# A hybrid decoder step on one core: two HGRN heads to a level's matmul, eight places for the last sequence's value pages

## The reference

```
f_t = lb + (1 - lb) sigmoid(z_t)
S_t = diag(f_t) S_{t-1} + (1 - f_t) i_t^T
o_t = S_t^T q_t
```

## Time and profile before

| what | value |
|---|---|
| median of three runs | 2284.1 us |
| the profiled execution's own time / its span | 2280.88 us / 2279.3 us |
| PE busy | 2039.0 us (89%) |
| DVE busy | 1647.4 us (72%) |
| ACT busy / POOL busy | 503.4 us (22%) / 199.6 us (9%) |
| moved by DMA | 356.42 MB, 156 GB/s on average |
| TensorE clock granted | 0.943 on average |

### The profile page before, as it was taken

The page is one execution under the profiler, slowest core; times in us unless marked ns, Lnnn a source line. Parts: engine busy times, 40 slices in busy tenths (PEclk is TensorE's granted clock), DMA queues, the critical chain, the costliest instruction groups (busy, mean ns, idle before and its releaser), DMA issues.

```text
span 2279.3 us, 30198 instructions
## 1 busy us (share of the span) xinstructions
PE 2039.0 (89%) x8954; PEld 1056.7 (46%) x8954; DVE 1647.4 (72%) x3478; ACT 503.4 (22%) x1248; POOL 199.6 (9%) x390
## 2 busy tenths in 40 slices
PE   6899899988899889687879998999999998999974
PEld 3445445544444445344445554455445554555340
DVE  2588777776777777577578877888688878888531
ACT  1233233433343334233101110111101111011100
POOL 0000121211111111110200000000000000000000
PEclk9999999999999999798979999999999999999966
DMA  6254455634443343543455553555355544555353
GB/s 216 98 163 159 158 195 187 195 138 143 154 143 121 120 134 122 188 176 113 157 166 170 172 167 129 172 171 180 102 190 168 173 162 136 178 164 171 112 177 117
DMA packets 167798, 356.42 MB, mean 156 GB/s; under 512 B 21040, under 2 KB 25920, under 8 KB 167648
## 3 DMA queue, kind: packets, MB, share of 16 engines
q1 hardware_dynamic: 136144, 248.80, 33.2%
q0 software_dynamic: 31504, 105.80, 13.8%
HBM read 322.52 MB, written 32.00 MB: 156 GB/s over the span
## 4 chain that ended last, share of the span: by engine, by line
PE 37%; DVE 9%; DMA 3%; SPq 2%; issue 2%; ACT 0%; DVEq 0%; ACTq 0%
PE PS L729 17%; PE PS L809 8%; PE PS L841 4%; PE PD L500 2%; DVE Kt L1306 2%; DVE sc L1311 2%; DMA Kt<-in_cache_k_dram 2%; DMA Vt<-in_cache_v_dram 1%; SPq L2025 1%; SPq L2018 1%; PE PO L861 1%; PE PO L862 1%; PE PS L867 1%; PE PS L914 1%; PE PT L743 1%
## 5 line engine op out<-in xcount | busy, mean ns | idle before, releaser
L399 PE MATMUL PT<-W,xT 128*128 128x512 f32 x960 | 436.2, 602 | 1.2 <-ACT xT L969 1.1
L1306 DVE TENSOR_TENSOR Kt<-Kt,qb 128x1024 f32<-128x1024 f32 x256 | 311.9, 1218 | 38.6 <-DMA Kt<-in_cache_k_dram 38.1
L1311 DVE TENSOR_REDUCE sc<-Kt 128x16 f32<-128x1024 f32 x256 | 312.2, 1219 | 8.0
L399 PEld LDWEIGHTS PT<-W,xT 128*128 128x128 f32 x960 | 178.7, 194 | 194.6 <-issue 192.6
L729 PE MATMUL PS<-W,xbuf 128*128 128x512 f32 (+1 forms) x576 | 263.0, 611 | 0.8 <-DVE oX L1607 0.8
L809 PE MATMUL PS<-region 128*128 128x512 f32 (+1 forms) x544 | 247.4, 599 | 0.8 <-ACT region L1184 0.8
L729 PE MATMUL PS<-W,xT 128*128 128x512 f32 x512 | 222.4, 592 | 0.0
L1006 ACT ACTIVATE Pr<-PS,negm 128x512 f32<-128x512 f32 (+7 forms) x192 | 165.3, 865 | 162.4 <-DVE negm L1325 144.7
L500 PE MATMUL PD<-Vt,pst 128*8 128x512 f32 x960 | 133.6, 629 | 60.2 <-DMA Vt<-in_cache_v_dram 60.2
L729 PEld LDWEIGHTS PS<-W,xbuf 128*128 128x128 f32 (+1 forms) x576 | 104.2, 186 | 140.5 <-issue 139.0
L444 PE MATMUL PS<-region,Q 64*128 64x512 f32 (+3 forms) x640 | 162.1, 621 | 0.0
(11 more groups left out here) (355 smaller groups left out, 2257.9 us busy)
## 6 DMA issues: line engine op xcount, KB each, us to landing
Kt<-in_cache_k_dram SPq DMA_DIRECT2D x512, 256.0 KB, 3.5
Vt<-in_cache_v_dram SPq DMA_DIRECT2D x288, 256.0 KB, 3.5
Vt<-in_cache_v_dram POOLq DMA_DIRECT2D x192, 256.0 KB, 4.3
W<-in_w_in_dram SPq DMA_DIRECT2D x4, 2048.0 KB, 19.0
xT_scratch<-xT POOLq DMA_DIRECT2D x16, 512.0 KB, 6.4
...
Kt<-in_cache_v_dram SPq DMA_DIRECT2D x32, 256.0 KB, 4.6
...
```

What stands on the lines that cost most here:

```text
L399: mm = pe.matmul(Pj, xT[:, c, :], W[:, b, c, :], start=(c == 0), stop=(c == DC - 1))
L1306: link(ve.tensor_tensor(kp, kp, qb[:, :].unsqueeze(1).to_broadcast([P, 2, G]), ALU.mult))
L1311: ve.tensor_reduce(sc[:, g % 2, bass.ds(r16, 2), :].rearrange("p a c -> p (a c)"), kp.rearrange("p a (c d) -> p (a c) d", d=64), X, ALU.ad ...
```

## The change

**Levels.** Heads 2 and 3 are computed in reversed order of time within a tile. Their early tokens then stand where heads 0 and 1 have late ones, so that one stationary tile of 128 columns holds the early keys of one head and of one mirrored head, and one moving tile the 64 + 64 late queries of both. A level from 1 on is two matmuls in place of four, and DVE's masked copy is 128 x 256 in place of 128 x 512. Level 0 stays as it was.

**What this asks for.** `xr` holds x with its columns reversed, made by ScalarE (ACT) in one 128 x 1024 copy to a tile (`mirror_x`), for the next tile behind `ib`. Each projection matmul of N = 512 becomes two of N = 256, one with x and one with xr. The copy of the transposed outputs (`yT_half`) turns two of the heads back, in two instructions where there was one. The masks are made anew by POOL: 28 `affine_select`s of 128 x 128 in pairs with a wait between, and eight small ones for the tail.

**The tail.** The states go to `W[:, 1]` and are issued after the tail's first projection. The value quads have eight places: `Vt`, `Kt`, and halves of `W` blocks 0, 3 and 2 as their projections end. SP issues the even quads and POOL the odd ones. PE transposes the HGRN half of the output (`y_half(0)`) between the last two groups of four quads, and multiplies that half by its weights (`tail_out(0)`) ahead of the attention half. In SP's stream the load of the states stands between the new wait on `proj` and quad 2.

The diff, cut to what matters (dedented; the tail's masked copy, semaphores and removed mask code are left out):

```diff
@@ -266,7 +265,8 @@
-masks = part(8 * P).rearrange("p (l t) -> p l t", l=8)
...
+near = part(4 * 2 * P).rearrange("p (l w) -> p l w", l=4)
@@ -275,6 +275,8 @@
+far = Pflat[:, 6 * G:6 * G + 3 * 2 * P].rearrange("p (l w) -> p l w", l=3)
+masks = [None] + [near[:, l, :] for l in range(4)] + [far[:, l, :] for l in range(3)]
@@ -282,6 +284,7 @@
+xr = normw[:, :].rearrange("p (c t) -> p c t", c=DC)
@@ -296,7 +299,8 @@
-SX = W[:, 0, :, :].rearrange("p c n -> p (c n)").rearrange("p (s v) -> p s v", v=P)
+tail_place = [Vt, Kt] + [W[:, n, 4 * u:4 * u + 4, :].rearrange("p (a c) n -> p a c n", a=2) for n in (0, 3, 2) for u in range(2)]
+SX = W[:, 1, :, :].rearrange("p c n -> p (c n)").rearrange("p (s v) -> p s v", v=P)
...
@@ -355,6 +359,14 @@
+def tail_quad(eng, kind, q):
...
+    _, numbers = nc.values_load_multi_w_load_instructions(pages[:, 16 * 28 + 4 * q:16 * 28 + 4 * q + 4], engines=[kind], min_val=0,
+                                                          max_val=vc.shape[0] - 1)
+    for u, page in enumerate(numbers):
+        eng.dma_start(tail_place[q % 8][:, u // 2, u % 2, :],
+                      vc[bass.ds(page, 1), :, :].rearrange("a t n -> t (a n)")).then_inc(t_load[q % 8], 16)
@@ -485,17 +497,17 @@
...
+        if g < 8:
+            ring = Vt
+            for half in range(2):
+                if g < 4:
...
+        else:
+            q = 4 * (it - 2 * NT) + s // 2
+            ring = tail_place[q % 8]
+            pe.wait_ge(t_load[q % 8], 64 * (q // 8 + 1))
@@ -724,9 +736,16 @@
+        if rows == P:
+            pe.wait_ge(xr_made, n + 1)
...
-            mm = pe.matmul(PS[0:rows, BANK[b], :], x[:, c, :], W[:, b, c, :], start=(c == 0), stop=(c == DC - 1))
+            if rows != P:
+                mm = pe.matmul(PS[0:rows, BANK[b], :], x[:, c, :], W[:, b, c, :], start=(c == 0), stop=(c == DC - 1))
+            else:
+                for a, rowsx in ((slice(0, 2 * P), x[:, c, :]), (slice(2 * P, G), xr[:, c, :])):
+                    mm = pe.matmul(PS[:, BANK[b], a], rowsx, W[:, b, c, a], start=(c == 0 and a.start == 0), stop=(c == DC - 1),
+                                   skip_group_check=True)
...
@@ -835,10 +857,15 @@
-            for h in range(H):
-                a = slice(h * P, (h + 1) * P)
-                lhs, rhs = (kT[:, a], qT[:, a]) if l == 0 else (Xl[l % 2][:, a], Xl[l % 2][:, a])
-                mm = pe.matmul(PS[:, 2 + l % 2, a], lhs, rhs, start=True, stop=True)
+            if l == 0:
+                for h in range(H):
+                    a = slice(h * P, (h + 1) * P)
+                    mm = pe.matmul(PS[:, 2, a], kT[:, a], qT[:, a], start=True, stop=True)
+            else:
+                late = Xl[l % 2][:, 2 * P:].rearrange("p (a i w) -> p a i w", a=2, i=2)
+                out = PS[:, 2 + l % 2, 0:2 * P].rearrange("p (a i w) -> p a i w", a=2, i=2)
+                for i in range(2):
+                    mm = pe.matmul(out[:, :, i, :], Xl[l % 2][:, i * P:(i + 1) * P], late[:, :, i, :], start=True, stop=True)
@@ -871,6 +898,13 @@
+    def tail_out(a):
...
+        for b in range(2):
+            for c in range(4 * a, 4 * a + 4):
+                mm = pe.matmul(PS[0:TR, b, :], yTs[:, c, 0:TR], Wo[:, c, b * G:(b + 1) * G], start=(c == 0), stop=(c == DC - 1))
+        return mm
@@ -930,16 +964,21 @@
-    with pe.Fori(2 * NT + 2, 2 * NT + 4) as it:
-        for s in range(0, SLOTS, 2):
-            value_quad(it, s, 8)
+    for s in range(0, SLOTS, 2):
+        value_quad(2 * NT + 2, s, 8)
+    pe.wait_ge(yB, after(NT + 1, ONE_ON))
+    y_half(0, TR)
+    for s in range(0, SLOTS, 2):
+        value_quad(2 * NT + 3, s, 8)
...
+    pe.wait_ge(yT_ev, after(2 * NT + 1, ONE_ON))
+    tail_out(0)
...
-    y_transposes(NT, TR)
-    for quarter in range(4):
-        out_quarter(NT, quarter, TR)
+    y_half(1, TR)
+    pe.wait_ge(yT_ev, after(2 * NT + 2, ONE_ON))
+    tail_out(1).then_inc(h_mm, 1)
@@ -1178,11 +1217,23 @@
+    def mirror_x(n):
...
+        act.wait_ge(x_in[n % 2], 16 * (n // 2 + 1))
+        act.activation(xr, xB[n % 2][:, :, ::-1], ACT.Copy).then_inc(xr_made, 1)
...
+            yT_half(t, a, rows)
...
+    def yT_half(t, a, rows):
+        act.wait_ge(y_tr, 2 * t + (a + 1))
+        yt = PT[:, a, 0:4 * rows].rearrange("p (c t) -> p c t", c=4)
+        if a == 0 and rows == P:
+            act.activation(yTs[:, 0:2, :], yt[:, 0:2, :], ACT.Copy)
+            act.activation(yTs[:, 2:4, :], yt[:, 2:4, ::-1], ACT.Copy).then_inc(yT_ev, 1)
+        else:
+            act.activation(yTs[:, 4 * a:4 * a + 4, 0:rows], yt, ACT.Copy).then_inc(yT_ev, 1)
@@ -1206,6 +1257,8 @@
+        if n + 1 < NT:
+            mirror_x(n + 1)
...
@@ -1254,12 +1308,13 @@
+    yT_half(NT, 0, TR)
...
-    yT_out(NT, TR)
+    yT_half(NT, 1, TR)
...
@@ -1740,17 +1791,23 @@
-                xl, q, k, p_, q_ = (halves(a, m) for a in (Xl[l % 2], qT, kT, PP, QQ))
...
-                ve.tensor_tensor(xl[:, :, 1, :], q[:, :, 1, :], p_[:, :, 1, :], ALU.mult)
-                ve.tensor_tensor(xl[:, :, 0, :], k[:, :, 0, :], q_[:, :, 0, :], ALU.mult).then_inc(x_lev, 1)
...
-                link(ve.tensor_tensor(q_[:, :, 0, :], q_[:, :, 0, :], p_[:, :, 1, m - 1:m].to_broadcast(shape), ALU.mult))
-                link(ve.tensor_tensor(p_[:, :, 1, :], p_[:, :, 1, :], p_[:, :, 0, m - 1:m].to_broadcast(shape), ALU.mult))
+                keys, queries = Xl[l % 2][:, 0:2 * P], Xl[l % 2][:, 2 * P:]
+                both = keys.rearrange("p (j two m) -> p j two m", two=2, m=m)
+                p_late, q_early = late_and_mirror(PP, m), early_and_mirror(QQ, m)
+                ve.tensor_tensor(compact(queries, m), late_and_mirror(qT, m), p_late, ALU.mult)
+                ve.tensor_tensor(two_views(both[:, :, 0, :], both[:, :, 1, :]), early_and_mirror(kT, m), q_early,
+                                 ALU.mult).then_inc(x_lev, 1)
...
+                shape = [P, 2, P // m, m]
+                v = PP.rearrange("p (j two m) -> p j two m", two=2, m=m)
+                last_late = two_views(v[:, 0:P // m, 1, m - 1:m], v[:, P // m:, 0, 0:1])
+                last_early = two_views(v[:, 0:P // m, 0, m - 1:m], v[:, P // m:, 1, 0:1])
+                link(ve.tensor_tensor(q_early, q_early, last_late.to_broadcast(shape), ALU.mult))
+                link(ve.tensor_tensor(p_late, p_late, last_early.to_broadcast(shape), ALU.mult))
...
@@ -1966,28 +2024,37 @@
-    pool.memset(masks[:, 1:8, :], 0.0).then_inc(b_made, 1)
...
-    pool.wait_ge(b_made, 3)
+    pool.memset(near, 1.0).then_inc(m_made, 1)
+    pool.memset(far, 1.0).then_inc(m_made, 1)
...
+    pool.wait_ge(m_made, 3)
...
+    def between(ap, first, last, step):
...
+        pool.affine_select(out=ap, in_=ap, compare_op=ALU.is_ge, fill=0.0, base=-first,
+                           pattern=[[0, copies], [-step, nj], [0, w]], channel_multiplier=1).then_inc(m_made, 1)
+        made_masks += 1
+        pool.wait_ge(m_made, made_masks)
+        pool.affine_select(out=ap, in_=ap, compare_op=ALU.is_ge, fill=0.0, base=last,
+                           pattern=[[0, copies], [step, nj], [0, w]], channel_multiplier=-1).then_inc(m_made, 1)
+        made_masks += 1
...
+        for mirrored in range(2):
+            v = masks[l][:, mirrored * P:(mirrored + 1) * P].rearrange("p (i j m) -> p i j m", i=2, m=m)
+            between(v, m * mirrored, m * mirrored + m - 1, 2 * m)
+    for l in range(1, 5):
...
+        v = tailmask[:, l - 1, :].rearrange("p (j two m) -> p j two m", two=2, m=m)
+        between(v[:, :, 1, :].unsqueeze(1), 0, m - 1, 2 * m)
+        pool.memset(v[:, :, 0, :], 0.0).then_inc(m_made, 1)
+        made_masks += 1
@@ -2003,12 +2070,20 @@
+    pool.wait_ge(k_used, after(8 * 2 * NT, TWO_FREE))
+    tail_quad(pool, mybir.EngineType.Pool, 1)
+    for q in (3, 5, 7):
+        pool.wait_ge(proj, 4 * NT + 1 + q // 2)
+        tail_quad(pool, mybir.EngineType.Pool, q)
...
+    for q in range(9, 16, 2):
+        pool.wait_ge(v_used, after(4 * 28 + q - 7, ONE_ON))
+        tail_quad(pool, mybir.EngineType.Pool, q)
...
@@ -2091,12 +2160,16 @@
-    sp.wait_ge(k_used, after(8 * 2 * NT, TWO_FREE))
-    slots(2 * NT, ORDER_TAIL)
-    sp.wait_ge(proj, 4 * (NT + 1))
+    sp.wait_ge(v_used, after(4 * 28, ONE_ON))
+    tail_quad(sp, mybir.EngineType.SP, 0)
+    sp.wait_ge(proj, 4 * NT + 1)
...
-    with sp.Fori(2 * NT + 1, 2 * NT + 4) as it:
-        slots(it, ORDER_TAIL)
+    for q in (2, 4, 6):
+        sp.wait_ge(proj, 4 * NT + 1 + q // 2)
+        tail_quad(sp, mybir.EngineType.SP, q)
+    for q in range(8, 16, 2):
+        sp.wait_ge(v_used, after(4 * 28 + q - 7, ONE_ON))
+        tail_quad(sp, mybir.EngineType.SP, q)
@@ -2109,20 +2182,47 @@
-def predicated(ve, l, t, a_lev, a_cp, Am, masks, PS, spare):
+def late_and_mirror(ap, m):
...
+    v = ap.rearrange("p (j two m) -> p j two m", two=2, m=m)
+    return two_views(v[:, 0:P // m, 1, :], v[:, P // m:, 0, :])
...
+def early_and_mirror(ap, m):
+    v = ap.rearrange("p (j two m) -> p j two m", two=2, m=m)
```

(45 more changed lines are left out.)

64 lines of the change are left out of this document (20 added, 44 removed).

## The result

Four runs of the changed kernel took 2214.6, 2217.7, 2221.0 and 2229.4 us, a median of 2219.3 us; four runs of the kernel before beside them had a median of 2285.1 us. The ratio is 0.972 (95% interval 0.969 to 0.975). The forecast was 2224 us. The profiled execution took 2214.55 us with a span of 2212.7 us, against 2280.88 and 2279.3 us before.

What follows compares the result with a forecast made beforehand. PE was taken to bound stage B's plain tiles, with DVE near. From the profiled 2280.9 us, 28 for stage B and 32 for the tail leave 2221, or 2224 beside the median; 2206 to 2247 holds 8 in 10.

Steps and rivals of the forecast that it cites:

- the 56.3 that was named as a sign of being wrong: Plain tiles of stage B were to take 57.0 to 57.5 us; under 56.3 would count against the prediction.
- Levels: Stage B on PE: each level from 1 on loses 0.445 us, 3.1 us a tile, 49.8 us in 16 tiles.
- Level 2: PE's stop for DVE in plain tiles grows by the 0.445 us that level 1 saves: 5.3 us given back.
- Quad 3: In plain tiles PE newly waits 0.4 to 0.9 us for value pages; 0.7 taken, 8.4 us in 12 tiles.
- Opening tiles: Stage B's four opening tiles, bound by DVE, gain 2.4 us each in place of 3.1: 2.8 us given back.
- Split projections: In stage B 64 records of N = 512 become 128 of N = 256: 0.3 us a tile, 5 us added.
- The rival on weight loads: Stage B's 1024 added loads each delay PE by 0.19 us: 195 us added, 2419 us in all; chance 0.07.
- Mirrors and masks: ACT's reversed copy, 1.07 us, is covered and costs nothing; POOL's masks delay stage B's start by 0, at most 4.5 us.
- Second queue: In the tail, a second issuing queue buys little; eight places filled by SP alone would give nearly the same time.
- (a): Tail: the 1.91 us wait before the quad at 2175.64 goes.
- (b): Tail: the last quads find their pages in place and run at full clock, so `d_close` comes 23.3 us earlier.
- (c): Tail, from `d_close` to the output projection's end: 27.7 us shrink by 5.4 (half clock) to 9.2 (full); 7 taken.

Runs made afterwards that it cites:

- k6_first: The changed kernel with SP issuing the pages of key slot 6 ahead of the next x in stage B: median 2214.4 us, ratio 0.969.
- split_only: The kernel before, with each stage-B projection matmul of N = 512 cut in two of N = 256 and nothing else: ratio 1.000.
- one_queue: The changed kernel with all sixteen quads of the tail issued by SP to the same eight places: median 2223.7 us, ratio 0.971.

## Why the prediction was right

The forecast was 60 us less, from stage B 28 and from the tail 32. The two profiles show 27.8 and 35.8. That 27.8 comes so near to 28 is partly luck: the 28 are for 16 tiles, and for the 15 behind the first the sum gives 26.2, of which 19.9 from the plain ones, where 18.2 were measured, and 6.3 from the opening ones, where this pair of profiles has 9.6. Plain tiles took 57.5 us on average; one took 56.14, under the 56.3 that was named as a sign of being wrong, but it had no stop at level 2 even before (58.00). By the prediction's own steps:

- **Levels: right.** L868 and L863 hold 448 and 128 records, 288 matmuls, and a level takes 0.45 us.
- **Level 2: right in size, not in form.** The sum has level 1's 0.445 us given back in each plain tile. From the start of level 0 to that of level 2 the twelve tiles took 101.1 us before and 101.1 after (8.43 us in the tile of the earlier trace rows, 8.33 in the one above), so the halving of level 1 gave nothing, as forecast. But the wait put down to DVE became shorter, not 1.5 us: the 0.32 us for `yT`, named as covered work, took the place of part of it. The idle times alone hide this. They add up to 12.3 us before and 14.8 after, 2.5 more where 5.3 were given back, because a stop also costs the overlap of the records around it: a level's records have 0.61 us, and what follows them without a stop starts after 0.45. `k6_first` confirms the cause.
- **Quad 3: right in kind, under-sized.** PE idles 0.93 us a tile (0.50 to 1.33; 11.2 us in twelve) where 0.7 were taken, just above the estimate's 0.9. From quad 2's start to quad 3's it is 6.95 us on average where the halved levels alone would leave 5.95, so the price is 1.0.
- **Opening tiles: right on average.** In the profiled pair they lose 3.2 us each, but they scatter with the clock; over nine such tiles with the levels of before and twenty-one with those of after (three with the mirror made twice) the means are 75.6 and 73.4 us: 2.2 us, where the sum gave 2.4 less 0.3. The wait of 0.94 us for DVE's last masked copy fell to 0.13 or less (up to 0.37 in other profiles), and quad 1 still waits 2.5 to 2.9 us. The copy's pitch is 0.32 us at five levels and 0.52 at two, where 0.34 was taken for all.
- **Split projections: right.** 0.16 us a tile measured, 0.3 taken. The rival on weight loads is excluded by `split_only`.
- **Mirrors and masks: right.** The copy takes 1.06 us reversed, the straight activation of the earlier trace rows 1.07. POOL's last mask instruction starts at 1122.98 us and DVE's key slot at 1124.16: no wait.
- **Second queue: right**, by `one_queue`.
- **Tail, (a) and (b): right.** From the end of stage B to that of the samples' outputs 97.9 us in place of 100.0, so 2.1 where 1.9 were taken; and from there to `d_close` 9.0 us in place of 33.1, so 24.1 where 23.3 were taken, at full clock as chosen.
- **Tail, (c): the step that missed.** "I take 7" stood between 5.4 with half clock and 9.2 with full. Measured were 9.5 (18.2 in place of 27.7): PE no longer stops for 5 us ahead of the second half, and its records run at full clock. The stated bounds of the tail, 25 to 34, were too narrow for the 35.8, because (c) had no value above 9.2 and (b) none above 23.3: it took a quad's stated duration of 1.04 us for its pace, and the last four quads have 0.89 from start to start (2182.58 to 2186.13).

The twelve plain tiles lost 18.2 us, 1.5 each. The terms as measured from start to start are -3.1 for seven levels, +0.4 for level 1, +1.0 for quad 3 and +0.2 for the split projections, and they give the same 1.5.
